# Two mixtures of experts in one stage each, and the first weights of two output products a stage ahead

## The reference, cut to what matters

```python
yx = jnp.concatenate([mlstm_group, conv_group], axis=-1) @ w_out + b_out     # output product, block 1
x = x + gate * rms_norm(yx)
h = modulate(rms_norm(x))
s = sigmoid(h @ w_router);  idx = top_k(s + b_router, 8)                     # 64 experts
for rows, weight, e in blocks_of_128(idx):                                   # rows sorted by expert, padded
    xb = h[rows]
    y = (silu(xb @ we_gate[e]) * (xb @ we_up[e])) @ we_down[e]
    acc[rows] += y * weight
out = acc + shared_expert(h)                                                 # block 1 only
```

## Time and profile before

| | us |
|---|---|
| median of three runs | 2835.58 |
| the profiled execution, device time | 2835.88 |
| its span in the profile | 2834.1 |
| PE busy in the span | 2621.9 (93%) |
| DVE busy | 1778.5 (63%) |
| ACT busy | 1301.6 (46%) |
| POOL busy | 1106.7 (39%) |

### The profile page before, as it was taken

How to read it: one execution, slowest core, us unless ns; L and a number is a source line. 1 busy time by engine, 2 the same in 40 slices (tenths; PEclk the granted TensorE clock), 3 DMA queues, 4 the chain that set the end, 5 groups by cost and what they waited for, 6 DMA issues and landing times. The chain is left out here.

```text
span 2834.1 us, 40811 instructions
## 1 busy us (share of the span) xinstructions
PE 2621.9 (93%) x12420; PEld 1968.6 (69%) x12421; DVE 1778.5 (63%) x2547; ACT 1301.6 (46%) x1848; POOL 1106.7 (39%) x1056
## 2 busy tenths in 40 slices
PE   6999988799899999999999968998999999977998
PEld 3445436585588888888888857865967877766786
DVE  3766757667677578777786656655634342557764
ACT  3320116631466477767775644156123332326653
POOL 1870014023566466666665630158201000006454
PEclk9999989899999999999999989999999999988999
DMA  8440010333588799899898765200312332438972
GB/s 298 135 156 1 30 60 1 131 121 136 194 297 274 226 315 331 297 318 336 273 353 276 248 176 169 68 1 1 63 45 67 89 89 68 171 127 311 316 227 44
DMA packets 187316, 484.60 MB, mean 171 GB/s; under 512 B 37484, under 2 KB 93344, under 8 KB 166456
## 3 DMA queue, kind: packets, MB, share of 16 engines
q1 hardware_dynamic: 143072, 372.83, 35.4%
q0 software_dynamic: 42592, 106.04, 15.6%
q10 hardware_dynamic: 1544, 4.33, 0.4%
HBM read 432.35 MB, written 95.69 MB: 186 GB/s over the span
## 5 line engine op out<-in xcount | busy, mean ns | idle before, releaser
L2226 PE MATMUL psum<-moe_high,moe_xg_high 128*128 128x512 f32 x960 | 389.4, 406 | 17.9 <-issue 17.9
L2228 PE MATMUL psum<-moe_high,moe_xg_low 128*128 128x512 f32 x960 | 377.7, 393 | 0.0
L2227 PE MATMUL psum<-moe_low,moe_xg_high 128*128 128x512 f32 x960 | 374.8, 390 | 0.0
L1640 DVE TENSOR_TENSOR moe_low<-moe_raw,moe_high 128x2048 fp32r<-128x2048 f32 x160 | 359.0, 2284 | 3.0 <-ACT moe_high L1624 1.5
L1624 ACT ACTIVATE moe_high<-moe_raw 128x2048 fp32r<-128x2048 f32 x160 | 297.9, 1920 | 10.3 <-DMA moe_raw<-in_w_e_up 8.6
L1616 POOL DMA_INDIRECT moe_landing<-moe_rows,moe_ig_now x124 | 224.7, 1812 | 109.4 <-POOL moe_ig_now L1613 91.4
L1613 POOL COPY moe_ig_now<-idx 128x1 int32 (+1 forms) x124 | 173.3, 1398 | 196.0 <-DVE moe_xg L1653 156.5
L2226 PEld LDWEIGHTS psum<-moe_high,moe_xg_high 128*128 128x128 f32 x960 | 181.5, 189 | 55.6 <-issue 21.6
L2228 PEld LDWEIGHTS psum<-moe_high,moe_xg_low 128*128 128x128 f32 x960 | 180.6, 188 | 42.9
L2213 PE MATMUL psum<-moe_high_down,moe_hid_high 128*128 x488 | 203.5, 417 | 7.0 <-DVE moe_hid_low L2304 7.0
L2227 PEld LDWEIGHTS psum<-moe_low,moe_xg_high 128*128 128x128 f32 x960 | 181.5, 189 | 35.9
(11 more groups left out here) (638 smaller groups left out, 5644.5 us busy)
## 6 DMA issues: line engine op xcount, KB each, us to landing
moe_raw<-in_we_gate SPq DMA_DIRECT2D x64, 1024.0 KB, 8.5
moe_raw<-in_we_up SPq DMA_DIRECT2D x64, 1024.0 KB, 12.0
moe_raw<-in_we_down SPq DMA_DIRECT2D x64, 1024.0 KB, 8.6
x<-in_w_ada POOLq DMA_DIRECT2D x16, 1024.0 KB, 5.6
x<-in_w_in SPq DMA_DIRECT2D x32, 512.0 KB, 6.3
moe_raw<-in_w_e_gate SPq DMA_DIRECT2D x16, 1024.0 KB, 9.5
moe_raw<-in_w_e_up SPq DMA_DIRECT2D x16, 1024.0 KB, 13.3
moe_raw<-in_w_e_down SPq DMA_DIRECT2D x16, 1024.0 KB, 9.6
```

Source lines behind the costliest of these rows:

```text
L1640: dve.tensor_tensor(self.low[:, at:at + 2048].bitcast(F32R), self.raw[r][:, part], hi, ALU.subtract).then_inc(self.w_low, 1)
L2226: pe.matmul(to, x_hi, R(of_k(w_hi, k)), start=(k == 0), stop=False)
L2227: pe.matmul(to, x_hi, R(of_k(w_lo, k)), start=False, stop=False)
L2228: last = pe.matmul(to, x_lo, R(of_k(w_hi, k)), start=False, stop=(k == KD - 1))
```

## The change

**Output products.** A new class `OutWeights` places the weights of an output product and their two parts, and can load and split the first pair of rows before `stage_out` begins. In block 1 all four pairs are loaded by SP in `stage_mix`, and ACT cuts the first pair there, behind its moves of unit 0. In block 2 the first pair is rows 4 and 5; it has its own place, is loaded at the start of `stage_branches`, and is cut and its rest taken in that stage's last unit. In `stage_out` the order of ACT and DVE is now weight pair n, then source pair n, and PE spreads the second column of block 1 behind the first pair's products.

**Mixtures.** The bodies of `stage_dispatch` and `stage_experts` become functions (`dispatch_programs`, `expert_programs`) that return one program for each engine; `stage_mixture` runs both in one block, with no barrier between them. SP loads experts 2 and 3 when the rows of block 0 have been placed. The blank store, its ACT instruction and the spare tensor are gone, and the counters with them are one lower; POOL's first two blocks stand ahead of its loop. DVE waits with the split that stood behind the first gather until both gathers have their index (`ig_set`), and places block 0 when the gather itself has landed, not when POOL has passed it on. In mixture 2 one split of expert 0 stands ahead of the lists. ACT waits for the shared expert's stores in front of the split of a down weight.

```diff
@@ stage_mix @@
+    s.out_weights = OutWeights(s, "out_1", s.A["w_out"][0], s.x_at + 8 * KD * D + 32, 0)
     with nc.Block() as block:
+        @block.sync
+        def _(sp):
+            for i in range(KD // 2):
+                s.out_weights.load(sp, i)
...
                     act.activation(to_hT(u, k), half(u, k), ACT.Copy, scale=gain(k)).then_inc(moved_a, 1)
+                if u == 0:
+                    s.out_weights.cut_first(act)
@@ OutWeights @@
+    def load(self, sp, i):
+        k = self.order[i]
+        sp.dma_start(self.pair(i), self.src[:, k:k + 2, :]).then_inc(self.landed[i], 16)
+    def cut(self, act, i, counter):
+        act.wait_ge(self.landed[i], 16)
+        k = self.order[i]
+        act.activation(self.R(self.high[:, k:k + 2, :]), self.pair(i), ACT.Copy).then_inc(counter, 1)
+    def rest(self, eng, i, counter):
+        k = self.order[i]
+        eng.tensor_tensor(self.R(self.pair(i, True)), self.pair(i), self.high[:, k:k + 2, :], ALU.subtract).then_inc(counter, 1)
@@ OutNorm.tensor @@
-        for k in range(0, KD, 2):
-            pe.wait_ge(self.w_ready, k // 2 + 1)
-            pe.wait_ge(self.src_ready, k + 2)
+        spread(0)
+        for n, k in enumerate(self.order):
+            if n == 0:
+                pe.wait_ge(self.weights.first_ready, 1)
+            else:
+                pe.wait_ge(self.w_ready, n)
+            pe.wait_ge(self.src_ready, 2 * n + 2)
             for i in range(4):
                 last = self.products(pe, i, (k, k + 1))
...
+            if n == 0 and self.shift:
+                spread(1)
@@ OutNorm.vector @@
+        if not self.weights.elsewhere:
+            self.weights.rest_first(dve)
+        for n in range(KD // 2):
+            if n:
+                self.w_part(dve, n)
+            self.src_part(dve, 2 * n)
+            self.src_part(dve, 2 * n + 1)
@@ dispatch_programs @@
-                mo.blank_y(act)
...
+            sp.wait_ge(mo.moved, 1)
+            for e in (2, 3):
+                mo.load(sp, e, e)
...
-                dve.wait_ge(first_out, 1)
-                if not side:
-                    mo.cut_low(dve, 0, 0, 0)
+            dve.wait_ge(mo.ig_set, 2)
             mo.cut_low(dve, 0, 0, 1)
-                mo.place(dve, 0, None)
+            mo.place_first(dve)
@@ expert_programs, scalar @@
+                    if b == 0 and mo.first_rows:
+                        mo.first_rows.wait_stored(act)
                     mo.cut_high_down(act, (b + 2) % 4, ep + (b >= 2))
@@ stage_mixture @@
+    with s.nc.Block() as block:
+        @block.sync
+        def _(sp):
+            lists[0](sp)
+            blocks[0](sp)
...
@@ stage_branches @@
+                follow.load(sp, 0)
                 for u in range(2, UNITS):
...
+                    if u == UNITS - 1:
+                        act.wait_ge(merged, u)
+                        follow.cut_first(act)
...
+                    if u == UNITS - 1:
+                        follow.rest_first(dve)
```

More of the change, by code:

```diff
@@ new lines, in sync @@
+        def sync(sp):
+            with sp.Fori(1, E // 4) as ep:
+                for b in range(4):
+                    after = first_block(sp, 4 * ep + b - 3)
+                    sp.wait_ge(gu_done, after + HEAD)
+                    mo.load_gate_up(sp, 4 * ep + b, b)
+                    sp.wait_ge(down_done, after + 1 + HEAD)
+                    mo.load_down(sp, 4 * ep + b, b)
+            if mo.follow:
+                after = first_block(sp, E - RAW + 1)
+                sp.wait_ge(down_done, after + 1 + HEAD)
+                mo.follow.load(sp)
+                end = first_block(sp, E)
+                sp.wait_ge(gu_done, end + HEAD)
+                mo.follow.load_x(sp)
+                mo.follow.wait(sp)
+                pairs = end >> 1
+                sp.wait_ge(added[0], 16 * (pairs + 2))
+                sp.wait_ge(added[1], 16 * (pairs + 1))
+                mo.follow.load_sums(sp, mo.accs)
@@ new lines, in expert_programs, with stage_mixture, _ @@
+        return sync, gpsimd, tensor, scalar, vector
+def stage_mixture(s, mo, gate, mask, start, idx, row_w, side=None):
+    with ExitStack() as routing:
+        if side:
+            side.hold(routing)
+        lists = dispatch_programs(s, mo, gate, mask, start, idx, row_w, side)
+    blocks = expert_programs(s, mo, start, idx, row_w)
+    with s.nc.Block() as block:
[3 more added lines that the diff above has]
+            blocks[0](sp)
+        @block.gpsimd
+        def _(pool):
+            lists[1](pool)
+            blocks[1](pool)
+        @block.tensor
+        def _(pe):
+            lists[2](pe)
+            blocks[2](pe)
+        @block.scalar
+        def _(act):
+            lists[3](act)
+            blocks[3](act)
+        @block.vector
+        def _(dve):
+            lists[4](dve)
+            blocks[4](dve)
```

843 lines of the change are left out of this document (413 added, 430 removed).

## The result

The changed kernel took 2819.91 us (median of 17 runs, 2810.34 to 2830.04) against 2833.8 us of the kernel before (17 runs, 2824.49 to 2839.76): a ratio of 0.9949, with an interval of 0.9935 to 0.9963. That is 14.4 us less (10.5 to 18.4). The forecast was 20.8 us less, 2815.1. A second series, of 11 runs, gave 0.9955 (0.9940 to 0.9970). The profiled execution took 2821.28 us, with a span of 2819.1.

A forecast was written before the change was run, and what follows sets the result against it. The prediction took PE to bound the kernel, busy 2621.9 of 2834.1 us. Four earlier starts, 4.2 + 6.5 + 4.6 + 5.5 = 20.8 us, taken from 2835.9 gave 2815.1 us, with a range of 2808 to 2827.

The forecast's parts named there:

- the entry that stays: Rival: PE's 3.1 us entry in mixture 1 stays unhidden, block 1's pair 0 at half clock; 15.9 us gained, 2820.0; chance 0.13.
- Block 1's output product: Term: PE's products in block 1's output product start earlier, with one spread ahead of them; 4.2 us, ends 1.0 and 5.6.
- Mixture 1's start: Term: without the barrier, PE's entry runs under the shared expert's products; first down product 6.5 us earlier, ends 3.5 and 7.4.
- nobody on PE waits for expert 2's cut: Mixture 1: ACT's cut of expert 2 follows block 0, and nobody on PE waits before that; priced at nothing.
- Block 2's output product: Term: first pair prepared in the stage ahead, then PE waits 2 to 3 us for pair 1; 4.6 us, ends 3.2 and 6.2.
- Mixture 2's start: Term: first gather alone and no barrier, block 0 6.3 us earlier; 5.5 us taken, ends 2.0 and 6.3.
- DMA takes mixture 2's part back: Rival: earlier loads meet the second gather, so mixture 2 gives 2.0 us or less; 17.3 in all, 2818.6; chance 0.12.
- slower: Rival: 80 loop entries in the mixtures lose their cover at 0.5 us each, 40 us against 20.8; 2855; chance 0.04.
- the entry and the second gather: Two signs of being wrong: PE's entry into the mixtures keeps 3 us; mixture 2's second gather lands after 2570.
- The third: Sign of being wrong: PE's idle time inside the mixtures grows; no size given.

The follow-up runs named there:

- mix_only: The kernel before with only the mixtures' part of the change, output products as before; 2823.49 us, ratio 0.9966.
- after: The changed kernel, first trace, with the whole change against the kernel before; 2819.91 us, ratio 0.9949.
- after_again: The changed kernel once more, unaltered, for a second trace and more timings; 2820.67 us, ratio 0.9955 to the kernel before.
- spread_ahead: The changed kernel with both column spreads ahead of the first pair in block 1's output product, traced twice; 2815.86 us, ratio 0.9945, in the second run.
- two_sums: The changed kernel with mixture 2's additions going alternately to the output and a second tensor, not added back; 2813.68 us, ratio 0.9931.
- barrier_back: The changed kernel with lists and experts of each mixture in two stages again; 2825.84 us, ratio 0.9966.
- barrier_again: A second trace of the changed kernel with lists and experts of each mixture in two stages again; no time given.
- entry_wait: The changed kernel with PE waiting in mixture 1 for ACT's last shared-expert move before entering the experts' program, without a barrier; no overall time given.
- before: The kernel before the change, first trace; 2833.8 us.

## Why the prediction came out as it did

The direction, the place and the order of the four gains were right, and the time lies within the range. The time alone would not show that: 2819.9 is nearer to two of the rivals (2820.0 for the entry that stays, 2818.6 for DMA in mixture 2) than to the forecast of 2815.1. Point by point, with the means of the table's traces:

- **Block 1's output product: 3.8 us** (A 152.1 in three traces without it, 148.3 in nine with it), 4.2 forecast. The first product came 20.9 us behind the start of `stage_mix` instead of 25.0, a gain of 4.2 against the 4.1 forecast. For the clock I took 1.9 us of a possible 3.0; pair 0 gained 2.8 us in four traces of nine and 0.9 to 1.2 in five, 1.8 in the mean. That the mean fits is luck: I had put the first spread at 3.1 us and the gap at 2.0, and they are 3.75 and 0.96, and which traces get the full clock is not set by the gap.
- **Mixture 1's start: 6.5 us** (B 111.4 in the three traces that have the mixtures of the kernel before, 105.0 in mix_only, after, after_again, the two of spread_ahead and two_sums), 6.5 forecast. The two traces of barrier_back and barrier_again stay out of it, as SP's loads make them worse. The down product came 7.5 us behind the last move, against 6.7 forecast, and PE waited 1.18 us for DVE's split as the step says. One sentence failed: that nobody on PE waits for expert 2's cut. The second block's down product waits 1.8 us for DVE, which waits for ACT, which waits for the load:

```profile
756.79 3.72 ACT L1690 ACTIVATE moe_high<-moe_raw 128x2048 fp32r<-128x2048 f32 x2 [3.52 <-DMA moe_raw<-in_we_up]
...
765.23 0.49 PE L2270 MATMUL psum<-moe_high_down,moe_hid_high 128*128 x1 [1.79 <-DVE moe_hid_low L2360]
```

- **Block 2's output product: 5.2 us** (D 136.1 to 130.9), 4.6 forecast. The gap behind pair 0 was 1.3 us, 2 to 3 forecast.
- **Mixture 2's start: 6.3 us** at block 0 (E 34.3 to 28.0), just as forecast, and the term of 5.5 had taken 0.8 off for DVE; the second gather was the slow one and held nothing up.

Together 21.8 us, 20.8 forecast. Measured were 14.4 and 12.8 us in the two series, with intervals that reach to 18.4 and 17. So the starts were priced well, and **what the sum had wrong** is that it counted them whole and put at nothing what the stretches behind them give back.

The reason for that stands against the rival "DMA takes mixture 2's part back", to which I gave a chance of 0.12: later loads are released by PE's own counters and move along with it. That is true of the loads; it is not true of the additions, each of which waits for the one before to land. In the changed kernel's first trace block 0 is 6.7 us ahead, and the tenth down product 0.1. The windows of F in that trace and in the kernel before, the kernel before first:

```profile
2573.60:2671.80 98.20, 95.08 (x447) 77.03 (x447) 82.24 (x74) 70.15 (x74) 57.76 (x38) 0.98 0.98 363
...
2551.20:2655.90 104.70, 97.60 (x446) 78.63 (x447) 84.61 (x75) 69.80 (x73) 46.40 (x39) 0.96 0.94 342
```

Of the 6.5 us that F is longer, 4.0 are idle time of PE, and 2.5 are the same matmuls at a lower granted clock. In mixture 1 it is the same: C is 6.8 us longer than in the kernel before, 3.9 of it idle (11.8 us against 7.8), and 3.0 more busy time of PE. The largest wait there, and its reason on ACT; the wait is for transfers of weights, which the forecast had at nothing:

```profile
1468.88 3.72 ACT L1690 ACTIVATE moe_high<-moe_raw 128x2048 fp32r<-128x2048 f32 x2 [2.48 <-DMA moe_raw<-in_we_up]
...
1474.25 1.91 ACT L1695 ACTIVATE moe_high_down<-moe_raw 128x2048 fp32r<-128x2048 f32 x1 [1.65 <-DMA moe_raw<-in_we_down]
...
1478.14 0.50 PE L2270 MATMUL psum<-moe_high_down,moe_hid_high 128*128 x1 [3.06 <-DVE moe_hid_low L2360]
```

And the windows up to that product and behind it:

```profile
1474.00:1478.00 4.00, 1.08 (x9) 0.80 (x7) 1.86 (x3) 3.75 (x5) 1.37 (x2) 1.00 1.03 422
1478.10:1486.00 7.90, 7.86 (x28) 6.33 (x29) 2.44 (x5) 1.98 (x4) 4.05 (x5) 0.78 0.86 269
```

The wait costs its 3.06 us, and then the clock falls to half for a part of the next 8 us. C of each trace of the changed kernel has two such falls, each behind a wait of 1.8 to 3.5 us; C of the two traces of the kernel before has none, although the second of them has waits of 1.7 and 1.8 us near the same two places.

How much of this the earlier start brings about is not shown. In the mean over the traces mixture 2 gave back 2.3 us of 6.3 and mixture 1 gave back 2.4 of 6.5, but these are the two differences of scattered values from above. Taken as they are they leave 17.1 us; the last 3 us or so are not resolved, and the stretches outside the table vary by more than that.

One slip in the rivals: with the lower ends of the output products the first rival's sum is 1.0 + 3.5 + 3.2 + 5.5 = 13.2, so 2822.7 and not 2824.

The rival "slower", by the cost of 80 loop entries, is out: PE's waits on `issue` in the loops are nine of 0.5 us at most, 4.5 in all, against ten with 5.0 in the earlier trace rows. The rival of the entry that stays is half right, in a way I had not put: the entry keeps its price (4.6 us where it is laid bare), but it is fully covered.

Of the prediction's own signs of being wrong, the entry and the second gather did not come (block 1's rows are placed at 2551.64, which is 2567.4 on the clock of the kernel before). The third did: PE's idle time inside the mixtures grew in the first trace, in C from 7.8 to 11.8 us and in F from 3.1 to 7.1.

What stays open is why the same kernel's inside of mixture 2 differs by 7.2 us between two executions, and so whether an earlier start makes that worse or the traces fell that way; and why the clock rises at one of two moments under the same work. It would take many more traces of each kernel.

## What to carry to other kernels

An earlier start is worth what is left of it at the end of the next stretch whose transfers are full. Look there for a chain in which one transfer waits for another to land, since such a chain need not keep the earlier start, and do not count the gain of such a stretch whole until several traces show it.
When a stage border goes, ask separately what the border costs and what the engine's own way into its next loop costs, and whether work is queued to run above the latter. And take no loss from a single trace of a stretch with full transfers: a second trace of the same kernel moved the two insides by 1.6 and 7.2 us. When a stretch with a busy PE has grown, split the growth into idle time and busy time of PE for the same count of matmuls: here 2.5 of 6.5 us were the clock.

## What the runs showed that I had not expected

- PE's way into the experts' loops costs 4.6 us when nothing runs above it (entry_wait), 3.1 behind a border (before), and nothing visible under the shared expert's products.
- Under the same work, the clock rose 3.7 us behind the start of a spread in four traces and 8.0 to 8.8 us behind it in five; the same 24 matmuls took 5.6 us, or 7.2 to 7.5.
- A wait of PE of 3.06 us inside mixture 1 was followed by a fall of the clock (0.78 in the next 8 us, 1.00 before it), and the same 4304 matmuls took 3 us longer in the two traces of the changed kernel than in the two of the kernel before.
- An indirect gather's issue takes 1.1 us on POOL by itself (1.04 to 1.14 in these traces) and 2.4 to 2.8 beside a DVE split of 2.29 us, whichever of two gathers it meets.
- An addition that waits for the one before it to the same tensor starts 7.2 to 7.5 us behind it in the last 80 us of the changed kernel (DMA share 0.30), and 14.0 behind it at 2597.84 (DMA share 0.99 from 2575 to 2620).
